# Order of the normalised halves, six kept down tiles and an earlier gate read in a two-layer decoder trunk

## The reference, cut to what matters

```python
for layer in range(2):
    hn = rmsnorm(x, norm_mix_g[layer])
    proj = hn @ w_in[layer]                    # columns for three mixers and the gates
    o_a = gated_deltanet(...)                  # 4 heads of 128, chunks of 64
    o_b = rwkv7_time_mix(...)                  # 8 heads of 64
    o_c = stick_breaking_attention(h_sb)       # 8 heads of 64, blocks of 128 queries
    gates = sigmoid(h_gate)                    # 3 x 1024 columns
    merged = sum(gates[i] * (o_i @ w_branch_i) for i in range(3))
    x = x + merged @ w_out[layer]
    hn = rmsnorm(x, norm_ffn_g[layer])
    if layer == 0:
        x = x + (silu(hn @ w_gate) * (hn @ w_up)) @ w_down          # hidden width 2816
    else:
        x = x + sum(combine[:, e] * swiglu(hn, expert e) for e in range(8))   # top 2 of 8
return rmsnorm(x, final_norm_g)
# attention, per block of queries, z = q k^T / 8, strictly causal:
#   log_a = log_sigmoid(z) + reversed cumsum of log_sigmoid(-z) - log_sigmoid(-z);  o = exp(log_a) @ v
```

## Time and profile before

| what | value |
|---|---|
| median of 3 runs | 2057.37 us (2057.05 to 2058.26) |
| profiled execution, its own time | 2054.16 us |
| its span | 2052.4 us |
| PE busy | 1962.2 us (96%) |
| DVE, ACT, POOL busy | 392.6, 271.1 and 88.2 us |
| mean DMA rate | 235 GB/s |

### The profile page before, as it was taken

How to read it: one execution, slowest core, us unless ns; L and a number is a source line. 1 busy time by engine, 2 the same in 40 slices (tenths; PEclk the granted TensorE clock), 3 DMA queues, 4 the chain that set the end, 5 groups by cost and what they waited for, 6 DMA issues and landing times.

```text
span 2052.4 us, 66808 instructions
## 1 busy us (share of the span) xinstructions
PE 1962.2 (96%) x31214; PEld 1742.7 (85%) x31214; DVE 392.6 (19%) x948; ACT 271.1 (13%) x579; POOL 88.2 (4%) x174
## 2 busy tenths in 40 slices
PE   7999999999999999999999799999999999999997
PEld 7888887888777788888788799999999898989896
DVE  3335331110000133533211300101000101010001
ACT  1223223000000122222320000000000000000001
POOL 4011101000000001011000000000000000000000
PEclk9999999999999999999999899999999999999999
DMA  7313123467442151311345389999999999999996
GB/s 239 123 44 102 43 84 103 144 207 244 144 144 82 42 160 47 101 45 43 107 139 204 137 335 407 407 407 407 407 407 407 407 407 407 407 407 407 407 407 240
DMA packets 214760, 482.92 MB, mean 235 GB/s; under 512 B 11582, under 2 KB 110092, under 8 KB 214668
## 3 DMA queue, kind: packets, MB, share of 16 engines
q1 hardware_dynamic: 214668, 481.54, 62.9%
HBM read 480.46 MB, written 1.05 MB: 235 GB/s over the span
## 4 chain that ended last, share of the span: by engine, by line
PE 83%; DMA 6%; SPq 4%; DVE 3%; ACT 1%; issue 1%; POOL 0%; DVEq 0%; POOLq 0%
PE bank L1190 29%; PE bank L623 18%; PE bank L1144 7%; DMA pool<-in_moe_w_down_dram 6%; PE bank L713 5%; PE bank L1071 4%; PE bank L1104 4%; SPq L2111 3%; PE bank L1087 3%; PE bank L636 2%; PE bank L677 2%; PE bank L1299 1%; SPq L2116 1%; PE bank L1034 1%; DVE pool L1814 0%
## 5 line engine op out<-in xcount | busy, mean ns | idle before, releaser
L1190 PE MATMUL bank<-pool 128*64 128x80 f32 x21504 | 759.5, 234 | 32.1 <-DMA pool<-in_moe_w_down_dram 23.5
L1190 PEld LDWEIGHTS bank<-pool 128*64 128x64 f32 x21504 | 752.6, 138 | 40.3 <-DMA pool<-in_moe_w_down_dram 25.8
L623 PE MATMUL bank<-hnT,pool 128*128 128x256 f32 x1856 | 431.5, 386 | 6.4 <-DVE pool L1876 6.4
L623 PEld LDWEIGHTS bank<-hnT,pool 128*128 128x128 f32 x1856 | 349.0, 192 | 61.7 <-issue 14.4
L1144 PEld LDWEIGHTS bank<-hnT,pool 128*128 128x128 f32 x640 | 121.6, 190 | 24.6 <-issue 9.1
L1144 PE MATMUL bank<-hnT,pool 128*128 128x256 f32 x640 | 141.2, 379 | 0.0
L2019 DVE TENSOR_TENSOR pool<-pool,bank 128x320 f32<-128x320 f32 x32 | 15.6, 488 | 637.4 <-ACT pool L1584 637.4
L713 PEld LDWEIGHTS bank<-pool 64*64 64x64 f32 x3008 | 94.8, 135 | 17.2 <-issue 11.3
L713 PE MATMUL bank<-pool 64*64 64x32 f32 (+2 forms) x3008 | 103.4, 221 | 2.6 <-DVE pool L1660 1.6
L1584 ACT ACTIVATE pool<-bank 128x320 f32<-128x320 f32 x32 | 14.0, 437 | 675.5 <-PE bank L1190 675.5
L561 POOL TENSOR_TENSOR pool<-pool,level_mask 128x256 f32<-128x256 f32 x72 | 51.9, 736 | 782.1 <-DVE pool L1736 502.1
(11 more groups left out here) (323 smaller groups left out, 1222.4 us busy)
## 6 DMA issues: line engine op xcount, KB each, us to landing
pool<-in_moe_w_up_dram SPq DMA_DIRECT2D x128, 896.0 KB, 16.6
pool<-in_moe_w_gate_dram SPq DMA_DIRECT2D x128, 896.0 KB, 16.6
pool<-in_w_in_dram SPq DMA_DIRECT2D x66, 1024.0 KB, 5.3
pool<-in_moe_w_down_dram SPq DMA_DIRECT2D x64, 1024.0 KB, 16.8
pool<-in_moe_w_down_dram SPq DMA_DIRECT2D x32, 1536.0 KB, 18.6
pool<-in_ffn_w_gate_dram SPq DMA_DIRECT2D x11, 1024.0 KB, 8.5
pool<-in_ffn_w_up_dram SPq DMA_DIRECT2D x11, 1024.0 KB, 5.7
pool<-in_ffn_w_down_dram SPq DMA_DIRECT2D x11, 1024.0 KB, 5.1
```

The lines of the kernel that those rows point to most:

```text
L623: ins = mm(ps[:, s * T:(s + 1) * T], w[:, k, (j + s) * P:(j + s + 1) * P], hnT[:, k, :], start=(k == 0), stop=(k == KD - 1))
L1190: ins = mm(bank[rows, cs], w[:, rows], rhs, start=start, stop=stop, skip_group_check=True)
```

## The change

At the start of each layer DVE turns the first half before it scales the second. In the dense stage six down tiles (f = 16 to 21) are kept for the end instead of three, and the count that DVE waits for before it adds t = 0 follows. In attention DVE copies gate tile 0 out behind heads 0 and 1, and PE puts 4 steps of filling instead of 5 before the values.

```diff
@@ attention, on TensorE
                     some(steps, 5)
                     sums(2 * j)
                     sums(2 * j + 1)
-                    some(steps, 5)
+                    some(steps, 4)
                     values(j)
@@ dense_ffn, on TensorE
-                        if f - 1 >= LAST - 2:
+                        if f - 1 >= LAST - 5:
                             kept.append(former)
                         else:
                             down_tile(*former)
@@ attention, on VectorE
-                opens = ((), (0, 1), (2,), (3,))
+                opens = ((0,), (1,), (2,), (3,))
@@ dense_ffn, on VectorE
-                    down_mm.wait(v, 0, down_mm.per_layer - 2 * (1 - t))
+                    down_mm.wait(v, 0, down_mm.per_layer - 3 * (1 - t))
@@ the layer's program, on VectorE
                 v.tensor_copy(vecs[:, l, 0:V_ROWS], proj[1][:, 0:V_ROWS]).then_inc(vec_ready, 1)
+                v.wait_ge(vec_ready, l + 1)
+                turned(l, 0, 0)
                 scaled(l, 0, 1)
-                v.wait_ge(vec_ready, l + 1)
-                for t in range(NT):
-                    turned(l, 0, t)
+                turned(l, 0, 1)
```

## The result

The changed kernel took 2043.54 us (median of 4 runs, 2042.85 to 2043.82) against 2057.21 us (4 runs, 2054.36 to 2058.26): ratio 0.9935, 95% interval 0.9918 to 0.9952. The forecast was 2046.5 us, range 2043.5 to 2051.5. The profiled execution took 2043.32 us with a span of 2041.6 us; the sum had given 2043.3 and 2041.5.

A forecast was written before the change was run, and what follows sets the result against it. TensorE was taken to bound the work before the experts, through idle holes and half-clock stretches, and the weight stream to pace the experts. Attention 9.8 plus layer starts 1.1 gave 10.9 us: 2057.4 to 2046.5 us, range 2043.5 to 2051.5.

The forecast's parts named there:

- the sum: Whole kernel: attention 9.8 plus layer starts 1.1 gives 10.9 us saved; profiled execution 2043.3 us, span 2041.5.
- The gate copy: Attention: copying tile 0 behind head 1 shrinks TensorE's hole from 3.20 to 0.2 us, 3.0 us saved a layer.
- the clock part: Attention, sums of heads 0 and 1: without the hole no clock fall, 1.64 us back a layer, bounds 0 and 1.7.
- a rival at 0.14: The clock gives nothing back: slow stretches reappear in the same stage or elsewhere; gain 7.6, time 2049.8 us; chance 0.14.
- Four steps: Attention: four filling steps before the last values remove TensorE's 0.28 us wait for POOL's mask, with no new wait.
- The layer starts: Start of each layer: turning before scaling starts TensorE 0.54 us earlier in layer 1, 0.56 in layer 0.
- the case weighed in the prediction: Layer 0's start: if the clock rises at the same instant, the 0.56 us head start is worth only 0.28.
- Six tiles: Dense stage's end: six kept down tiles gain 0 and cost 0, since the norm factor was already hidden.
- the rival at 0.07: Layer 1's first matmuls: the slow start shortens too, 1.3 to 2.5 us more, about 2044.5 us; chance 0.07.
- The stream rival: Expert stage: weight stream settles at 399 instead of 407 GB/s, 15.4 us longer, time 2061.9 us; chance 0.04.
- The offset of 3.2 us: Whole kernel: median of runs taken to lie 3.2 us above the profiled execution, as in the kernel before.

The follow-up runs named there:

- experiment 2: The kernel before with only gate tile 0 copied behind heads 0 and 1, steps left at 5: 2046.85 us, ratio 0.9961.
- experiment 4: The kernel before with 7 unread products a layer filling TensorE's wait behind the gate copy: 2052.72 against 2056.05 us, ratio 0.9986.
- experiment 6: The kernel before with only six down tiles kept instead of three: 2056.46 against 2055.38 us, ratio 1.0006.
- Experiment 7: Changed kernel with layer 1's first-half norm moved behind the addition of t = 0; against the kernel before: six kept tiles 2037.99 us (0.9910), three 2034.35 us (0.9901).
- before again: The kernel before, unchanged, timed and profiled once more: 2056.23 against 2056.98 us, ratio 0.9997; profile span 2055.4 us.
- experiment 1: The kernel before with both attention edits alone (gate copy and four steps): 2046.08 against 2055.38 us, ratio 0.9956.
- experiments 1, 5 and 6: Against the kernel before: both attention edits alone, ratio 0.9956; first half turned before second is scaled, alone, 0.9996; six kept down tiles alone, 1.0006.

## Why the prediction was right, and where it was not
- **The gate copy** was right in mechanism and size: 0.22 us idle where 0.2 was forecast, 1.74 us for the sums, 4.66 us a layer by experiment 2 where 4.64 was summed. That the clock part hangs on the hole, a rival at 0.14, is settled by experiment 4.
- **Four steps** were worth 0.35 us instead of 0.28, and no later values waited. Where the 0.07 more come from is not shown.
- **The layer starts** were right as starts (0.54 us in layer 1). In layer 0, copy to matmul was 2.28 us and is 1.73 (0.55); another 0.5 us came from the table's rows arriving earlier (copy at 10.79 instead of 11.32), which no edit does. The 32 records took 6.01 us after 5.33, and the block of 96 began at 19.24 instead of 19.65: of 1.08 us of head start 0.41 were left in this execution. That is the case weighed in the prediction, but the two profiles of the unchanged kernel differ as much (5.33 and 6.29 us for these records), so this pair can't show what the head start is worth.
- **Six tiles** were worth 0, by experiment 6, for the reason given: the first half's norm was held by DVE's order, not by its cover. Experiment 7 confirms it from the other side: with the order changed, the hole of 5.13 us goes (5.3 us less, as the first matmul slightly overlaps the last down tile), first matmul to block of 96 goes from 5.85 to 5.07 us, and the dense stage grows by 0.99 us of moved transposes: 5.1 us net.
- **Layer 1's slow start** got shorter as well, the rival at 0.07: clock 0.76 after 0.58, and from the last down tile to the block of 96 it is 10.98 us instead of 12.56, of which 0.53 is the hole and about 1.03 the clock. The sum had left this out. The changed kernel's second profile has 11.09 us. The seven profiles with the old order and a hole lie between 12.28 (before again) and 13.90 (experiment 1, whose hole is 6.62 us), and the turn alone has 12.00. So it changes from execution to execution, but both profiles of the changed kernel lie below all eight of these; whether the edits do that was not settled.
- **The experts** kept their length: 869.05 us after 870.21, and 871.19 in the unchanged kernel's second profile. The stream rival is out.
- **The total** came out 3 us below the forecast and inside the range by 0.04 us, which is luck. That the profiled pair met the sum, 10.8 us to 10.9, is luck in part as well: the attention stages give 10.0, layer 0's start 0.41 and layer 1's start 1.57, together 12.0 us; the draws ahead of the scores took 3.3 back, and the stretch to the experts and the experts themselves gave 2.1, which no edit explains.
- **The offset of 3.2 us** is the term that was mis-sized. The profiled execution of the kernel before lay 3.2 us under its median, and the forecast took the same for the changed kernel, whose profiled execution lay only 0.2 us under its own. The offset belonged to one execution: the unchanged kernel's second profile has a span 3.0 us longer. The medians show 13.7 and 13.5 us in the two comparisons (the interval of the second is 10.5 to 16.0 us). The edits timed alone add up to only 8.6 us (9.0, 0.8 and -1.2 in experiments 1, 5 and 6), each give or take 2 to 3 us. How the 1.5 us or more above the 12.0 split between the edits and the draw stays open.

## What to carry to other kernels
Look for a copy out of a bank that stands in its engine's queue behind work it does not need: the hole that it tore in TensorE here, 3.0 us, cost another 1.65 us at half clock behind it. More cover for a chain was worth nothing here until the engine that held the chain was told to take it up earlier; move the work first, then ask how much cover it needs (here three tiles were nearly as good as six). Where the clock's falls move from execution to execution by 2 to 3 us, compare stages of several profiles and not one span with a median.

## What the runs showed of the hardware
TensorE's clock fell to half in stretches in which it was busy throughout: in the windows of 80 to 92 us above it was busy 12.00 of 12.00 us with clock 0.72 and 0.86. Ahead of the fall ran products of one column each (L768) and of 8 columns. In the profile before they ran at clock 1.00, and the fall came behind them, at the transposes (L784) and projections (L623); in the profile after it came while they still ran. First the two windows before, then a window and the timeline after:

```profile
79.70:83.40 3.70, 3.70 (x34) 3.70 (x34) 0.34 (x2) 1.78 (x4) 0.00 (x0) 1.00 0.58 200
85.10:88.40 3.30, 3.30 (x14) 3.03 (x13) 1.64 (x7) 0.31 (x2) 0.00 (x0) 0.50 0.00 0
```
```profile
82.00:88.80 6.80, 6.80 (x34) 6.80 (x34) 1.99 (x10) 0.66 (x4) 0.00 (x0) 0.50 0.00 0
```
```profile
79.78 4.11 PE L768 MATMUL bank<-ones,pool 128*128 128x1 f32 x28
83.75 0.57 PE L772 MATMUL bank<-stat,incl 128*128 128x8 f32 x2
84.17 0.57 PE L773 MATMUL bank<-stat,same_chunk 128*128 128x8 f32 x2
```

The Trainium skill (TensorE: Matmul & The Clock Gate, Why this matters for your kernels) advises to leave no long idle gaps between bursts of matmuls. Experiment 4 agrees, 1.7 us a hole. These windows show that a profile's busy time is not enough to judge by: the profile counts TensorE as busy throughout, and the clock fell all the same. Whether the width of the products is the cause was not tried.
